# Prompt mixing in another unit order: first key head from wide to narrow, keys and values replaced in four groups, memory loads in seven parts

## The reference, cut to what matters

```
# B: attention over the selected keys, per 128-query block; 8 query heads share 2 key heads
s = q . k * B_HD**-0.5 ; s = where(selected and key <= query, s, -inf)
p = softmax(s) ; o = p @ v
# A: matrix memory, 4 heads, chunkwise; C (state) is carried from one tile of 128 tokens to the next
S = (q k^T) * decay ; num = S @ v + w_inter * (C q) ; C = w_prev * C + v^T (w_s * k)
```

## Time and profile before

| | us |
|---|---|
| median of 3 runs (lowest, highest) | 4092.59 (4086.96, 4095.04) |
| profiled execution, its own time | 4096.27 |
| its span in the trace | 4094.7 |
| the mixing phase in it, from the first load to the last store | 2195 to 3128 |

### The profile page before, as it was taken

One profiled execution on the slowest core, in us unless ns is written; L12 is line 12 of the kernel. 1 busy time (PEld: TensorE's weight loads), 2 busy tenths in 40 slices (PEclk: granted clock), 3 DMA queues, 4 the chain that ended last, 5 costly groups with the idle time before them and its releaser, 6 DMA issues. The chain is left out here.

```text
span 4094.7 us, 56203 instructions
## 1 busy us (share of the span) xinstructions
PE 3799.0 (93%) x21590; PEld 2365.7 (58%) x21590; DVE 2997.0 (73%) x4154; ACT 1414.6 (35%) x2401; POOL 1669.3 (41%) x1529
## 2 busy tenths in 40 slices
PE   7899999999999999999996897778977899999999
PEld 4555555554466566656664665555645688854444
DVE  5599999699999999999993665545555577753333
ACT  5312111264324444333322665455543222211111
POOL 0000045469777666665552211123202666552111
PEclk9999999999999999999997899889988899999999
DMA  5311232420121212111215432164232755541111
GB/s 218 93 65 52 77 96 83 148 73 36 70 70 46 70 63 69 69 62 62 69 62 125 136 90 65 52 146 125 72 102 87 213 167 167 162 149 56 45 57 45
DMA packets 307376, 379.98 MB, mean 93 GB/s; under 512 B 73531, under 2 KB 233619, under 8 KB 303910
## 3 DMA queue, kind: packets, MB, share of 16 engines
q1 hardware_dynamic: 266714, 260.48, 21.4%
q0 software_dynamic: 19664, 86.31, 5.8%
q10 hardware_dynamic: 20736, 29.66, 2.3%
HBM read 245.79 MB, written 129.28 MB: 92 GB/s over the span
## 5 line engine op out<-in xcount | busy, mean ns | idle before, releaser
L1315 DVE MAX8 best<-score 128x8 f32<-128x384 f32 (+13 forms) x448 | 639.6, 1428 | 23.4 <-POOL score L1283 8.5
L1317 DVE MATCH_REPLACE8 score<-best,score 128x384 f32<-128x384 f32 (+13 forms) x448 | 631.1, 1409 | 0.0
L1761 PE MATMUL mix_slot<-mix_kT,early 128*128 128x512 f32 (+3 forms) x640 | 294.1, 583 | 81.2 <-DMA early<-mask_scr 30.4
L1773 PE MATMUL mix_po<-mix_ring,mix_v 32*128 32x128 f32 x8704 | 276.6, 284 | 87.8 <-issue 74.7
L1773 PEld LDWEIGHTS mix_po<-mix_ring,mix_v 32*128 32x128 f32 x8704 | 268.0, 199 | 103.0 <-issue 102.4
L1072 PE MATMUL pr<-xnT,w_row 128*128 128x347 f32 (+1 forms) x960 | 298.3, 457 | 0.0
L396 PE MATMUL pg<-xnT,wt 128*128 128x416 f32 x800 | 281.8, 515 | 0.0
L1224 POOL TENSOR_TENSOR kT<-kT 128x347 f32<-128x347 f32 (+1 forms) x240 | 194.0, 808 | 214.8 <-ACT kT L1142 208.0
L1072 PEld LDWEIGHTS pr<-xnT,w_row 128*128 128x128 f32 x960 | 180.2, 189 | 106.5 <-issue 10.0
L1997 DVE CUSTOM_DVE_ANT_0 mix_ring<-mix_slot,early 128x512 f32<-128x512 f32 (+3 forms) x128 | 82.0, 640 | 213.6 <-PE mix_slot L1761 212.1
L1591 POOL DMA_DIRECT2D ybt_scr<-early x31 | 24.4, 788 | 522.9 <-ACT early L1899 522.9
(11 more groups left out here) (626 smaller groups left out, 7935.4 us busy)
## 6 DMA issues: line engine op xcount, KB each, us to landing
gt_scr<-kT SPq DMA_DIRECT2D x40, 694.0 KB, 3.3
out_gm<-gt_scr ACTq DMA_DIRECT2D x32, 520.0 KB, 4.7
gt_scr<-kT SPq DMA_DIRECT2D x20, 692.0 KB, 4.1
wt<-in_w_in SPq DMA_DIRECT2D x22, 512.0 KB, 4.1
w0a<-in_w_in SPq DMA_DIRECT2D x11, 1024.0 KB, 6.7
w_row<-in_w_in SPq DMA_DIRECT2D x10, 1024.0 KB, 6.7
qt_scr<-kT POOLq DMA_DIRECT2D x8, 1040.0 KB, 4.2
early<-ybt_scr SPq DMA_DIRECT2D x4, 2080.0 KB, 9.5
```

Source lines behind the costliest of these rows:

```text
L1315: nc.vector.max(best[:, :], sc).then_inc(top_step, 1)
L1317: nc.vector.match_replace(sc, best[:, :], sc, TAKEN).then_inc(top_step, 1)
L1761: mm(s[:, 0:width], bq[p][:, hh, :], kT[:, lo:lo + width], start=True, stop=True).then_inc(slot_mm, 1)
L1773: ins = mm(po[:, a, 0:GQ * BLK], v[rows, b, :], at[rows, :, BLK * b:BLK * b + BLK], start=b == 0, stop=b == blocks - 1)
```

## The change: what it does

1. **Unit order.** Key head 0 goes from block 15 down to block 0, key head 1 from block 0 up to 15 with block 8 taken out and put last.
2. **Ring.** `ring_places` tries for each unit the ends of the ring and the edges of the last four units and takes the place whose last overlapped unit is earliest. `ahead`, the number of units that may wait for their `O`, is 2 for i under 8 and 1 above.
3. **Keys and values.** Both have a semaphore for each group of four blocks. Group g of key head 1 is loaded after the unit (0, 4g): keys after its scores, values after its `O`. A score piece waits for its own group, a product too.
4. **Memory loads.** Tile m's loads (m from 2) are seven events `F m 0` to `F m 6` in heads 8m - 12 to 8m - 6: four of queries and keys, one of the decay, two of values.
5. The first projection weights of the next phase (4 MB) are loaded in four parts instead of one.

The core of the diff:

```diff
-MIX_UNITS = [(kv, i) for kv in range(KV) for i in range(NB)]
+MIX_UNITS = [(0, i) for i in range(NB - 1, -1, -1)] + [(1, i) for i in range(NB) if i != NB // 2] + [(1, NB // 2)]
...
-    at, after, cursor = [], [], 0
-    for u, (_, i) in enumerate(MIX_UNITS):
-        size = GQ * (i + 1) * P
-        if cursor + size > RING_COLS:
-            cursor = 0
...
+    for u in range(len(MIX_UNITS)):
+        size = unit_columns(u)
...
+        edges = {0, RING_COLS - size}
+        for w in range(max(0, u - 4), u):
+            edges |= {at[w] + unit_columns(w), at[w] - size}
+        place = min((lo for lo in edges if 0 <= lo <= RING_COLS - size), key=lambda lo: (last_shared(lo), lo))
+        after.append(last_shared(place))
+        at.append(place)
...
+    for m in range(2, NB):
+        for x in range(7):
+            at[8 * m - 12 + x] = at.get(8 * m - 12 + x, []) + [("F", m, x)]
...
-        ahead = 2 if u == 0 or 0 < i < 6 else 1
+        ahead = 2 if i < 8 else 1
...
+            def load_memory_part(i, x):
+                p, rows = i % 2, slice(i * P, (i + 1) * P)
+                if x == 0:
+                    after_slot(sp, ("M4", i - 2, AH - 1))
+                if x < 4:
+                    a, t = divmod(2 * x, AH)
+                    sp.dma_start(aqk[p][:, a, t:t + 2, :], d["qt"][2 * x:2 * x + 2, :, rows].rearrange("t p q -> p t q")).then_inc(qk_loaded[p], 16)
+                elif x == 4:
+                    sp.wait_ge(dmat_ready, i - 1)
+                    load_decay(sp, i)
...
+            load_queries(0)
+            load_keys(0, 0)
+            load_first_memory(0)
             for done, count in mask_stored:
                 sp.wait_ge(done, count)
-            load_a(0)
-            load_keys(0, 0, FIRST_KEYS)
-            load_v(0)
-            load_values(0, 0, FIRST_KEYS)
-            load_a(1)
-            load_m(1)
-            load_keys(0, FIRST_KEYS, NB)
-            load_values(0, FIRST_KEYS, NB)
+            load_mask(0)
+            for g in range(1, KEY_GROUPS):
+                load_keys(0, g)
+            load_first_values(0)
+            load_queries(1)
+            load_mask(1)
+            for g in range(KEY_GROUPS):
+                load_values(0, g)
+            load_first_memory(1)
+            load_decay(sp, 1)
+            load_first_values(1)
...
+                    kv, i = MIX_UNITS[u]
+                    if kv == 0 and i % KEY_GROUP == 0:
+                        after_slot(sp, e)
+                        load_keys(1, i // KEY_GROUP)
...
+                elif e[0] == "O" and MIX_UNITS[e[1]][0] == 0 and MIX_UNITS[e[1]][1] % KEY_GROUP == 0:
+                    sp.wait_ge(o_mm, e[1] + 1)
+                    load_values(1, MIX_UNITS[e[1]][1] // KEY_GROUP)
...
+                    pe.wait_ge(k_resident[kv][q], 16)
```

More of the change, by code:

```diff
@@ L1369, in key_pieces, with unit_columns, last_shared @@
     return len(pieces(head_width(n), 512))
+def unit_columns(u):
+    return GQ * (MIX_UNITS[u][1] + 1) * P
 def ring_places():
-    at, after, cursor = [], [], 0
-    for u, (_, i) in enumerate(MIX_UNITS):
-        size = GQ * (i + 1) * P
-        if cursor + size > RING_COLS:
-            cursor = 0
-        shared = [w for w in range(u) if at[w] < cursor + size and cursor < at[w] + GQ * (MIX_UNITS[w][1] + 1) * P]
-        at.append(cursor)
-        after.append(max(shared, default=-1))
-        cursor += size
+    at, after = [], []
+    for u in range(len(MIX_UNITS)):
+        size = unit_columns(u)
+        def last_shared(lo):
+            return max((w for w in range(u) if at[w] < lo + size and lo < at[w] + unit_columns(w)), default=-1)
+        edges = {0, RING_COLS - size}
[4 more added lines that the diff above has]
+        at.append(place)
     return at, after
@@ L1523, in prompt_mixing_phase @@
         po, pb = ps("po", [P, QUADS, 512]), ps("pb", [P, 512])
-        k_resident, v_resident = ([sem(f"{n}_resident{x}") for x in range(2 * KV)] for n in "kv")
+        k_resident, v_resident = ([[sem(f"{n}_resident{kv}{g}") for g in range(KEY_GROUPS)] for kv in range(KV)] for n in "kv")
         state_init = sem("state_init")
@@ L1618, in load_a, with load_mask, load_keys, load_values @@
                     after_slot(sp, last_piece(u - 2))
-                queries = d["qt"][lo:lo + GQ, :, rows].rearrange("t p q -> p t q") if i else d["first"][:, lo:lo + GQ, :]
-                for dst, src in ((bq[p], queries), (mk[p][:, 0:(i + 1) * P], d["mask"][i, :, 0:(i + 1) * P])):
-                    sp.dma_start(dst, src).then_inc(a_loaded[p], 16)
-            def load_keys(kv, lo, hi):
-                at = slice(lo * P, hi * P)
-                sp.dma_start(kT[:, at], d["qt"][T_BK + kv, :, at]).then_inc(k_resident[2 * kv + (lo > 0)], 16)
-            def load_values(kv, lo, hi):
+                src = d["qt"][lo:lo + GQ, :, rows].rearrange("t p q -> p t q") if i else d["first"][:, lo:lo + GQ, :]
+                sp.dma_start(bq[p], src).then_inc(a_loaded[p], 16)
+            def load_mask(u):
+                p, i = u % 2, MIX_UNITS[u][1]
+                sp.dma_start(mk[p][:, 0:(i + 1) * P], d["mask"][i, :, 0:(i + 1) * P]).then_inc(a_loaded[p], 16)
+            def load_keys(kv, g):
+                at = slice(g * KEY_GROUP * P, (g + 1) * KEY_GROUP * P)
+                sp.dma_start(kT[:, at], d["qt"][T_BK + kv, :, at]).then_inc(k_resident[kv][g], 16)
+            def load_values(kv, g):
+                lo, hi = g * KEY_GROUP, (g + 1) * KEY_GROUP
                 col = R_BKV + KV * HD + kv * HD
@@ L1755, in score_piece @@
                 p, (kv, i) = u % 2, MIX_UNITS[u]
-                if hh == 0 and q == 0:
-                    pe.wait_ge(a_loaded[p], 32 * (u // 2 + 1))
-                    pe.wait_ge(k_resident[2 * kv + (i >= FIRST_KEYS)], 16)
+                if hh == 0:
+                    if q == 0:
+                        pe.wait_ge(a_loaded[p], 32 * (u // 2 + 1))
+                    pe.wait_ge(k_resident[kv][q], 16)
                 lo, width = pieces(head_width(n), 512)[q]
```

64 lines of the change are left out of this document (27 added, 37 removed).

## The result

The changed kernel takes **4019.0 us** (4014.5 to 4031.3) beside 4092.4 for the kernel before: ratio 0.983, interval 0.980 to 0.985, 73 us off. The forecast, 4069 in a range of 4038 to 4095, had the sign right and was 50 us too high.

What follows compares the result with a forecast made beforehand. PE was taken as the bound of the 933 us mixing phase, its idle time and half-clock work as winnable. Terms -25.4 - 6 - 1.5 + 6 + 3 = -23.9 took 4096.3 to 4072.4 profiled, less 3.7: 4069 us, range 4038 to 4095.

Steps and rivals of the forecast that it cites:

- Term 1: Behind pairs of wide units: waits before `O 12` and `O 14` go, 22.4 us, plus 3 of half clock; -25.4 us.
- term 2: Phase start: waits 45 against 46.7 us, including 17 for tile 1, and 4.3 less half clock; -6 us.
- term 3: Switch of key head: 11.5 us of waits go, 10 of new waits for keys and decays come; -1.5 us.
- term 4: Products stopping in the middle: more of them, as transfer bursts now start with each product; +6 us.
- term 5: The rest: one more memory tile opening in a wide unit makes PE wait for `sd`; +3 us.
- half clock: PE work at 1.2 GHz: 3 us less behind the two removed pair waits, 4.3 less at the start.
- The tail has one wait, as now: End of the phase: the last unit's transposes lie under `O 30`, 16 us long, so no wait is added.
- the DMA queue frees more: Rival: tile 1 and decays arrive in time and no product stops; -52 us, 4040 us, chance 0.15.
- No change: Rival: two pair waits go, but bursts under products and the start give them back; +1, 4094 us, chance 0.15.
- slower: Rival: the decay is late in every narrow tile, tiles 5 to 12; +25 us, 4118 us, chance 0.13.

Runs made afterwards that it cites:

- e12: The changed kernel run again unaltered, in a later set of runs: 4039.8 us, ratio 0.986 to the kernel before.
- e13: The changed kernel run a third time unaltered, in another later set: 4037.4 us, ratio 0.986 to the kernel before.
- e10: The kernel before, with transposes of units 12, 14, 28 and 30 placed head by head among the next unit's scores: 4066.2 us, ratio 0.994.
- e15: The changed kernel with block 8 of the second head in its natural place, run beside e13: 4045.8 us, ratio 0.989 to the kernel before.
- e1: The changed kernel with the old unit order, the second head's four groups loaded behind unit 15: 4093.4 us, ratio 1.001 to the kernel before.
- e4: The kernel before, with 3 MB of its first values issued behind unit 3's loads: 4089.0 us, ratio 1.000.
- e11: The changed kernel with head 0 in the order 0, 1, 2, 15 to 3, so narrow units start: 4092.5 us, ratio 0.998 to the kernel before.
- e2: The changed kernel with all the second head's keys and values loaded behind unit 15 and `O 15`: 4037.6 us, ratio 0.988 to the kernel before.
- e17: The kernel before, with SP holding loads issued around the end of scores of units 18 to 26 until the next product: 4078.1 us, ratio 0.997.

## Why the prediction was wrong

The step that failed is the set of new waits that terms 2 to 5 put against the removed ones. The prediction had 16.6 us of idle time go in all; 60.1 went in the first trace, and 57.9 and 52.6 in e12 and e13. The switch was charged 10 us of new waits (3, 3 and 4) and PE waits there for neither keys nor decay; tile 1 was charged 17 us and cost 9.4; one more wait for `sd` of 3 us was charged and three of 3.2 went. Term 1, the largest in the sum, was right.

On the profiled executions the forecast was -23.9 us, and the phase, as counted in the table above, became 81.3 shorter. The last two columns are the same program in its two repeats. By the prediction's own steps:

| step | forecast | measured | e12 | e13 |
|---|---|---|---|---|
| term 1, waits of pairs | -22.4 | -19.7 (45.6 to 12.39 + 13.55) | -20.0 | -19.7 |
| term 2, waits at the start | -1.7 | -9.0 (46.7 to 37.6) | -9.7 | -10.0 |
| term 3, switch | -1.5 | -11.5 | -11.5 | -11.5 |
| term 4, stopping products | +6 | -2.2 (26.5 to 24.3) | -0.8 | +4.6 |
| term 5, waits for `sd` | +3 | -9.5 | -9.5 | -9.5 |
| waits in no term | 0 | -8.2 | -6.4 | -6.5 |
| half clock (in terms 1 and 2) | -7.3 | -22.6 | -10.6 | -8.9 |
| work | 0 | +1.3 | +9.9 | +10.1 |

- **Term 1** was right in mechanism and size. e10 gains 23.5 us from four spread pairs, and e15 loses 8 to one uncovered one. "The tail has one wait, as now" came out: 13.55 us before `O 29`, and the last unit's transposes lie under `O 30`. What the prediction did not price is what this is worth: with block 8 in its natural place the second head has three uncovered waits, 11.7, 12.7 and 13.1 us in e15, in place of two.
- **Term 2.** The 17 us for tile 1 were mis-sized: 5.65, then 3.70 for its `sd`. That the wide start is only neutral in waits was the larger error: up to a work of 80 it is worth 15 us of idle time and 4 of half clock. e1, e4 and e11 show the other side, narrow starts that wait 17 to 21 us behind the values. (The upper bound of the forecast's own range leaves out this term's +12, with which it ends at 4087 and not 4083.)
- **Term 3.** The 3 and 4 us for the decays of tiles 8 and 10 never came, nor the 3 for keys 0. I had the landing right (11 us) and charged 4 us to issue 1 MB, which took 1.93; the two products beside it covered the rest. e2 shows that with 4 MB in one go such a wait does come, 15.8 us.
- **Term 4.** I said that stops come "when a burst of transfers runs under a product" and charged more of them, because products would now start at SP's issues. e17 bears out the first half, and each stop ends behind an instruction packet. The second half stays open: the stops sum to 24.3, 25.7 and 31.1 us in three traces of one program, against 26.5 in the one of the kernel before, and in the last two the same matmuls also take 10 us more of work, in pieces. So the +6 was too high in the first trace and, if that longer work is counted with it, too low in the others.
- **Term 5.** The `sd` waits of 3 us are one of the pair's costs: a tile that opens in the second of two wide units whose scores run back to back. e1 and e10 keep such pairs and keep these waits (3.05 and 3.02 us the first ones); the new order has none beyond the start. That the product between gives ACT and DVE time to catch up is argued from the list, not tried. The five issues a tile that this term names are four, three transfers having become seven; so are the 70 more transfers 56. Neither is in the sum.
- **The half clock** was the largest single miss in the first trace, 15 us, and only 3 and 2 us off in e12 and e13. I took 1.5 us behind each removed wait, read behind one wait. But in the first traces of both kernels the stops of 4 to 8 us inside products are followed by work at 0.50 as the pair waits are. Behind the stop of rows 11, windows of the kernel before:

```profile
2845.50:2853.20 7.70, 0.00 (x0) 0.00 (x0) 5.22 (x5) 2.62 (x4) 0.94 (x1) 0.80 0.67 238
2853.20:2857.00 3.80, 3.79 (x72) 3.79 (x76) 0.00 (x0) 0.00 (x0) 0.00 (x0) 0.51 0.17 64
2857.00:2859.50 2.50, 2.50 (x77) 2.34 (x73) 0.00 (x0) 0.23 (x1) 0.00 (x0) 1.00 0.04 7
```

The product's 72 records take 3.8 us at 0.51, then 77 take 2.5. Over the phase 22.6 us went for 60 of idle time, 0.38 for each, near the 7.3 for 16.6 that I had priced; in e12 and e13 it was 10.6 for 57.9 and 8.9 for 52.6, under 0.2, so this is no rate to carry. What all three traces share is the idle time: too few waits were counted as the pairs', the switch's and the narrow start's.

The rivals: "the DMA queue frees more" came nearest. It had the decays right and tile 1 half right (5.65 us late), was wrong that no product would stop, had no term for the `sd` waits, and gave 4040. That the two repeats took 4040 and 4037 is luck in part, for they reach it with 10 us of longer work that it does not have. "No change" and "slower" rested on stops and decays that did not come; e2 is the kernel in which the second would have started. What stays open: why `O 18` and `O 20` run slowly in most later traces and not in the first ones, on one chip even and not by DMA load alone, and how the second head's 20 us divide between parts, ring and order.

## What to carry to other kernels

When a resource is filled once at the start, let the unit with the most work per byte come first: the same transfers cost 17 to 21 us of waiting behind narrow units and 6, then 4 more for `sd`, behind a wide one. When a reorder removes a wait, count its companions too, the short waits of the engines that were late with it and the half clock behind each, and look for them in the trace by the same pattern before adding new costs. The size of the half clock is no constant: two traces of one program differed by 12 us of it. Compare variants in one set of runs: the same program moved by 20 us between sets.

## What the runs showed of the hardware

- The instruction queue moves 83 packets of 16 KB in this phase beside the data. In the twenty traces 84 of 85 stops of over 2 us inside products end 1.2 to 1.6 us behind the landing of one. In one of them, with the DMA engines 66% busy, none moved for 4.4 us, and PE stood 7.8 us in the middle of a product; holding the loads took such stops from 19.0 us to 1.4.
- One product of 32-row matmuls took 3.0 us or 10.6 us for the same 96 records. The DMA share was 0.18 and 0.66 there, but another trace has 3.0 us at 0.73, so the share does not decide it.
- In the first traces of both kernels all seven waits before the products of pairs, and all six stops of 4 to 8 us inside products, are followed by work at a granted clock of 0.50. Behind one stop 72 records took 3.8 us at 0.51, then 77 took 2.5 at 1.00.
- One program took 4019, 4040 and 4037 us in three sets, while the kernel before moved only from 4090 to 4097.
